# Second block's attention: q and k split into high and low parts stacked over 128 rows, two rounded matmuls for a score in place of one plain one

## What is computed

```python
q = rms_norm(q.reshape(b, s, N_KV_HEADS, Q_PER_KV, HEAD_DIM), q_norm[i])
k = rms_norm(k.reshape(b, s, N_KV_HEADS, HEAD_DIM), k_norm[i])
q = axial_rope(q, ang_row, ang_col)
k = axial_rope(k, ang_row, ang_col)
...
sc = jnp.einsum("bqkgd,bskd->bkgqs", q_blk, k).astype(jnp.float32) * scale
p = jax.nn.softmax(sc, axis=-1).astype(v.dtype)
return jnp.einsum("bkgqs,bskd->bqkgd", p, v)
```

## Time and profile before

| | |
|---|---|
| median of 3 runs | 2386.71 us (2380.06 to 2392.92) |
| the profiled execution's own time | 2394.19 us |
| its span, first to last instruction | 2392.4 us |
| PE busy | 2241.5 us, 94% of the span |
| DVE, ACT, POOL busy | 1159.7, 990.6, 968.7 us |
| mean granted clock of TensorE | 0.954 |

### The profile page before, as it was taken

The page is one execution under the profiler, slowest core; times in us unless marked ns, Lnnn a source line. Parts: engine busy times, 40 slices in busy tenths (PEclk is TensorE's granted clock), DMA queues, the critical chain, the costliest instruction groups (busy, mean ns, idle before and its releaser), DMA issues.

```text
span 2392.4 us, 28135 instructions
## 1 busy us (share of the span) xinstructions
PE 2241.5 (94%) x10837; PEld 1836.2 (77%) x10848; DVE 1159.7 (48%) x1843; ACT 990.6 (41%) x1994; POOL 968.7 (40%) x750
## 2 busy tenths in 40 slices
PE   7999899999988897899999999996899999999997
PEld 6788778888877786788888887663587887888886
DVE  3445565553345764565553353555655335444322
ACT  5656444443235554244442254542344334332221
POOL 3555553434455651544343432214432334232232
PEclk9999999999989998899999987997999999999998
DMA  4112123232222221122323211110012232222221
GB/s 154 53 54 71 53 88 105 89 105 83 97 77 89 80 71 36 53 88 88 106 86 108 80 64 36 36 36 18 18 45 79 91 106 82 92 90 104 99 97 51
DMA packets 29845, 183.08 MB, mean 77 GB/s; under 512 B 3984, under 2 KB 4112, under 8 KB 11920
## 3 DMA queue, kind: packets, MB, share of 16 engines
q1 hardware_dynamic: 29712, 181.27, 22.0%
HBM read 174.97 MB, written 2.10 MB: 74 GB/s over the span
## 4 chain that ended last, share of the span: by engine, by line
PE 85%; DVE 6%; ACT 4%; issue 3%; POOL 1%; DMA 1%; SPq 0%; another core or an unknown queue 0%; POOLq 0%; ACTq 0%; DVEq 0%
PE PS L1346 83%; PE PS L1471 1%; POOL LO L2582 1%; PE PS L1583 1%; DVE bQS L2049 1%; DVE cCVT L2458 0%; DMA RAW<-wall 0%; DVE aQS L2049 0%; DVE T_f L2121 0%; PE PS L1519 0%; DVE XL L2126 0%; DVE YH L2151 0%; ACT HI L1671 0%; POOL bTQ L2640 0%; ACT bP L1887 0%
## 5 line engine op out<-in xcount | busy, mean ns | idle before, releaser
L2582 POOL TENSOR_TENSOR LO<-RAW,HI 128x512 fp32r<-128x512 f32 (+2 forms) x382 | 539.5, 1428 | 633.2 <-ACT HI L1671 633.2
L1346 PE MATMUL PS<-XH,HI 128*128 128x512 f32 (+1 forms) x1584 | 642.6, 406 | 29.2 <-DVE XL L2049 6.7
L1346 PE MATMUL PS<-XH,LO 128*128 128x512 f32 (+1 forms) x1584 | 625.7, 395 | 0.0
L1346 PE MATMUL PS<-XL,HI 128*128 128x512 f32 (+1 forms) x1584 | 619.7, 395 | 2.2 <-DVE XL L2126 2.1
L1671 ACT ACTIVATE HI<-RAW 128x512 fp32r<-128x512 f32 (+3 forms) x668 | 365.6, 608 | 171.2 <-PE PS L1346 168.0
L2049 DVE TENSOR_TENSOR LO<-RAW,HI 128x512 fp32r<-128x512 f32 (+2 forms) x286 | 304.6, 1069 | 248.2 <-ACT HI L1671 247.8
L1346 PEld LDWEIGHTS PS<-XH,HI 128*128 128x128 f32 (+1 forms) x1584 | 302.6, 191 | 113.1 <-issue 41.9
L1346 PEld LDWEIGHTS PS<-XH,LO 128*128 128x128 f32 (+1 forms) x1584 | 301.7, 190 | 65.8 <-issue 0.8
L1346 PEld LDWEIGHTS PS<-XL,HI 128*128 128x128 f32 (+1 forms) x1584 | 302.1, 191 | 62.9 <-DVE XL L2126 3.7
L1346 PE MATMUL PS<-HH,HI 128*128 128x512 f32 x528 | 205.4, 389 | 0.0
L1346 PE MATMUL PS<-HL,HI 128*128 128x512 f32 x528 | 205.4, 389 | 0.0
(11 more groups left out here) (378 smaller groups left out, 3396.8 us busy)
## 6 DMA issues: line engine op xcount, KB each, us to landing
RAW<-wall SPq DMA_DIRECT2D x138, 1024.0 KB, 4.8
RAW<-wall SPq DMA_DIRECT2D x24, 896.0 KB, 4.4
bROT<-bTQ SPq DMA_DIRECT2D x64, 64.0 KB, 2.0
RAW<-wall SPq DMA_DIRECT2D x5, 512.0 KB, 3.3
XF<-xT SPq DMA_DIRECT2D x4, 512.0 KB, 5.3
outT<-XR SPq DMA_DIRECT2D x8, 256.0 KB, 2.0
FP<-cfp SPq DMA_DIRECT2D x1, 1024.0 KB, 7.2
MKF<-cmask SPq DMA_DIRECT2D x1, 704.0 KB, 11.0
```

Of the source, the lines that this page charges most:

```text
L1346: return e.matmul(out, a, b, start=start, stop=stop)
L2582: return e.tensor_tensor(out, x, h.bitcast(F32), ALU.subtract)
```

## The change

A new step `cqs` stands after each block's `cr3`, with a yield of its own. For a block of q, ACT copies the two heads' halves rounded (`Copy` into F32R, 64 x 512 each) and DVE writes the two remainders into the other 64 partitions of the same tiles, so that cQS[h] has the high part in one half and the low part in the other. For k, ACT writes the high part of each key head into both halves (four copies), DVE the two low parts into cKL. A score is then one product over 128 rows (high and low q with high k) and one over 64 rows (high q with low k), both rounded, into one bank. The scores of a head wait for `cqs` of its block and no longer for `cr3`. The new tiles lie on cQ blocks that are no longer needed and on tiles of the state-space branch, which adds two waits: ACT's in `cqs` for n = 2, 3, and DVE's in `cxm` for j = 8.

```diff
+    "cqs": (("qh", 1), ("ql", 1)),
...
         def rotated(n):
             put("cr3", n)
+            yield
+            put("cqs", n)
             turned_q[n] = True
             yield
...
+    cQS = [None] * 8
+    for at, off in enumerate([E0 + 38 * K + 512 + 2 * K * i for i in range(4)] + [E0 + 2 * K * n for n in (0, 4, 1, 2)]):
+        cQS[HEADS[at]] = sb(f"cQS{HEADS[at]}", 512, F32R, off)
+    cKH = [sb(f"cKH{g}", 512, F32R, R0 + 117 * K + 2 * K * g) for g in range(2)]
+    cKL = sb("cKL", 512, F32R, E0 + 36 * K)
...
             elif kind == "csc":
                 h, i = a
                 if i == 0:
-                    e.wait_ge(*when("rotp", "cr3", h % 4 or 4))
-                r = slice(64 * (h // 4), 64 * (h // 4) + 64)
-                mm(PS[bank][:, :], cQ[r, 512 * (h % 4) + 128 * i:512 * (h % 4) + 128 * i + 128], cQ[r, 2048:2560]).then_inc(SEM["qk"], 1)
+                    e.wait_ge(*when("ql", "cqs", h % 4 or 4))
+                g, q = h // 4, blk(cQS[h], i, 128)
+                r = slice(64 * g, 64 * g + 64)
+                mm(PS[bank][:, :], q, cKH[g][:, :], True, False)
+                mm(PS[bank][:, :], q[r, :], cKL[r, :], False, True).then_inc(SEM["qk"], 1)
...
+            elif kind == "cqs":
+                n, = a
+                e.wait_ge(*when("rotp", "cr3", n))
+                if n in (2, 3):
+                    e.wait_ge(*when("ql", "cqs", n - 1))
+                for x in range(2):
+                    r = slice(64 * x, 64 * x + 64)
+                    m = act((cKH[x] if n == 4 else cQS[n + 4 * x])[r, :], cQ[r, 512 * n:512 * n + 512], ACT.Copy)
+                    if n == 4:
+                        m = act(cKH[x][64 - 64 * x:128 - 64 * x, :], cQ[r, 2048:2560], ACT.Copy)
+                m.then_inc(SEM["qh"], 1)
...
+            elif kind == "cqs":
+                n, = a
+                e.wait_ge(*when("qh", *step))
+                for x in range(2):
+                    r = slice(64 * x, 64 * x + 64)
+                    if n == 4:
+                        m = diff(cKL[r, :], cQ[r, 2048:2560], cKH[x][r, :])
+                    else:
+                        m = diff(cQS[n + 4 * x][64 - 64 * x:128 - 64 * x, :], cQ[r, 512 * n:512 * n + 512], cQS[n + 4 * x][r, :])
+                m.then_inc(SEM["ql"], 1)
...
             elif kind == "cxm":
                 j, = a
+                if j == 8:
+                    e.wait_ge(*when("qk", "csc", 5, 3))
```

## The result

The changed kernel takes 2379.45 us (median of 19 runs, 2375.34 to 2387.25), the kernel before 2386.71 (19 runs beside them): a ratio of 0.9968, 95% interval 0.9955 to 0.9981. That is 7 us less where 9.2 were predicted, inside the range of 2366 to 2390 and within 0.5%. Another 9 runs gave 0.9951 (0.9934 to 0.9968).

The account below looks back on a forecast made before the run. PE was taken to bound the stage up to 1632, with small waits. The terms -13.6 + 1.4 + 0.5 + 3.0 + 0.9 + 0.0 - 1.4 sum to -9.2, taking 2386.71 to 2377.5 us; range 2366 to 2390.

Parts of the forecast that it names:

- Scores, -13.6: Attention scores on PE: new product pair saves 0.39 us in 30 at full clock, 0.94 in two at half; 13.6 less.
- The first rival: Scores: the 64-row low product costs only 0.23 us, so scores give -22.1 and the total is 2369 us; chance 0.25.
- Key's split, +1.4: First score: PE waits 1.4 us for the key's copies and subtractions, 3.9 us long with 2.6 covered.
- Block 1, +0.5: Block 1's copies on ACT, ahead of the step sizes' conversion, lengthen PE's wait for a copied transpose by 0.5 us.
- Block 3, +3.0: Block 3's subtractions on DVE, directly ahead of head 4's copy cPT, make a v product wait 3.0 us (bounds 0, 7.2).
- +0.9 for the clock: Behind block 3's wait the clock may fall, costing 1.7 us; half of that is taken, 0.9.
- Ends of units, 0.0: Waits ending cx 0 to cx 4: +2.7 at cx 0, +0.1 over cx 1 to cx 3, -1.1 and -1.7 at cx 4.
- the -1.4 at cx 5: End of cx 5: result copy and POOL's work go ahead of ACT's turn of the last heads, 1.4 us less (bounds 0, 2.56).
- The slower rival: New waits keep the clock at half through cx 0: net +19 us, 2405 us; chance 0.10.
- the sign set for being wrong: Wrong if PE waits for the convolutions instead, or if the granted clock in cx 0 is under 0.7.

Follow-up runs that it names:

- products alone: Kernel before with each score as a 128-row and a 64-row rounded product, no split, steps and waits unchanged: 2374.88 us against 2388.62, ratio 0.9942.
- split alone: Changed kernel with the whole split but the old plain f32 64-row product as score: ratio 1.0012 to the kernel before.
- Order alone: Kernel before with only the extra yield and an emptied new step, so attention stands one step later: ratio 0.9973 to the kernel before.
- the last split: Changed kernel with the last block's split seven steps later in the list (eight yields ahead instead of one): ratio 0.9952 to the kernel before.

## Why the prediction was right, and where its terms were off

The forecast of -9.2 was met at -7.6 (ratio 0.9968) and -11.7 (0.9951). By its own steps:

- **Scores, -13.6: right at full clock.** The starts are those given, 0.23, 0.33 and 0.43 to 0.01 us, and the two timed comparisons gave 13.9 (products alone, 8 to 20) and 10 to 15 (against split alone). At half clock the pair took 0.21, 0.64 and 0.73 (1451.45 to 1453.03), 1.58 in place of the 1.41 given. The first rival, a short product at no extra cost, is out by the same rows; its saving per score is to be had, but with 128 rows.
- **Key's split, +1.4: too small.** The first product's chain was taken from POOL's addition on, with PE as slow as in the one profile seen. In an execution with an early full clock PE is there 6 us sooner, and block 0's split delays the key's rotation in ACT's queue on top. The wait measured 7.9 and 8.8 there and 2.0 to 3.4 with a late clock. Since the kernel before waits 3.1 in the first case, the split's own part is some 5 and 2 to 3. The sum also has no term for the clock behind this wait: in the changed kernel's two profiles 14 us ran at half from the wait on.
- **Block 1, +0.5: about right.** PE's wait for ACT's cPT was 2.10 against 1.92, 0.2 more.
- **Block 3, +3.0, and +0.9 for the clock: place and chain right, the clock too small.** The wait was 1.7 and 4.0, at the v product, with the two subtractions directly ahead of the copy, as said. But 19 us at half clock stood behind it in both profiles against 6 with the split moved away, and against 7, 14 and 7 at the end of cx 0 in the kernel before, which has no such wait. So some 5 to 12 of the 19 go with the wait. The price of a clock fall was taken from the earlier trace rows, where linear products followed. Here 5 us of the decays' 16-column products, and transposes, stood among them, and the next wait (cCU, 2.9) came before the clock was back; that this is the reason is argued, no run varies it.
- **Ends of units, 0.0.** cx 0 2.88 (predicted 3.2), cx 1 to cx 3 0.53, 0.54, 0.53 (0.8 each), cx 4 1.18 (1.15), without a fall of the clock: 1.00 over the 6 us behind it where before had 0.72. A little better than said. Order alone, with 3.8 us in parts II and III, against 4.1 from the same terms, agrees with them and the -1.4 at cx 5 together.
- **By parts.** The steps sum to +4.3 in part I and -13.5 in II and III. Measured: +4 to +9 and -11.9. The shortfall of 1.6 in II and III is nearly all the scores': from split alone to the changed kernel, with the same order, the 24 gave 8.1, 0.34 each and not 0.39, and PE's wait for cBT took 0.4 of the difference (1.47 against 1.10). No term had the wrong sign. That the total came out so close is in part luck: two terms of part I were too small, and whether that shows as +4 or as +9 hangs on the clock of the executions compared.
- **The slower rival** was partly right: 14 us of cx 0 and the first 5 of cx 1 ran at half clock, with PE busy 16.1 of the 19. That is 8 us of work at full rate, or 9 of cx 0 at its 0.90, near the 11.5 from which the rival has the gain gone. The mean granted clock over cx 0 was 0.73 and 0.81 in the two profiles (0.90 before), so the sign set for being wrong, under 0.7, was not reached, but nearly.

What stays open: how much of part I's clock loss a median over executions sees. The profiles of the last split put 6 to 8 us on it and its wait, the timed runs 0 to 4. Nor do the runs show why the clock comes back after 7 us in one execution and 41 in another.

## What to carry to other kernels

A product with half its rows costs its neighbours time: if the other half can be filled with something that is wanted or harmless, fill it. Cheap work for idle engines is not free when it lands in a queue ahead of something that the busy engine waits for next: put it as late as its reader allows. And price such a wait with the busy engine at its fastest, not as the one profile shows it, and count what its clock does afterwards.

## What the runs showed of the hardware that was not expected

- In all fourteen profiles the granted clock fell to 0.50 among the same products with 2 columns and stayed there for 7 to 41 us, by execution and not by kernel; in the first profile of the kernel before PE was busy 33.9 of 34.0 us in it. The stage took 227.6, 227.6 and 227.7 us in three executions of one kernel all the same.
- A rounded product over 64 rows starts 0.09 us late and makes the next start 0.2 late, at full clock; over 128 rows neither (0.23 each). Its load takes no longer (0.183 against 0.188), but starts with its own product where a 128-row load starts with the product ahead.
- Every wait of 2 us or more for the first score came with a half-clock stretch of its own: 14, 14, 14, 10 and 27 us with waits of 7.9 to 8.8, and 3 to 10 us with those of 2.0 to 3.6. With one of 0.75 there was none.
- A wait of 1.7 us was followed by 19 us at 0.50, with PE busy 16.1 us of them. One of 2.27, at the start of cx 5, was followed over 6 us by 0.72 in each of three profiles of the kernel before, by 0.50 with the products alone and by 1.00 without the yield.
